# Gate pairs: high parts of the weight blocks first, weight sums in SBUF, gate tiles in two places by turns, all spatial products in the first pair

## The reference

```python
mq, mk, mv, mo, mi, mf, su, sv, wq, wk, wv, gl = split_in(h @ p['w_in'])
...
y_sg, v_norm = spatial_gating(su, sv, ...)      # u * (w_spatial @ layer_norm(v) + b)
...
gates = jax.nn.sigmoid(gl).reshape(B, S, N_BRANCH, D_MODEL)
merged = (gates[:, :, 0] * (y_ml @ p['w_br_mlstm'])
          + gates[:, :, 1] * (y_sg @ p['w_br_gmlp'])
          + gates[:, :, 2] * (y_sw @ p['w_br_swa']))
x = x + g1 * rms_norm(merged @ p['w_out'], p['g_post_mix'])
```

## Time and profile before

| | |
|---|---|
| median of three runs | 2094.71 us |
| profiled execution, its span | 2096.62 us, 2094.8 us |
| PE busy | 2031.4 us (97%) |
| PE weight load busy | 1956.9 us (93%) |
| DVE, ACT, POOL busy | 1088.8, 685.9, 1025.6 us |
| mean granted TensorE clock | 0.990 |
| HBM traffic | 100 GB/s over the span |
| chain that ended last | PE 84%, DVE 5%, issue 3%, DMA 3% |

### The profile page before, as it was taken

How to read it: one execution, slowest core, us unless ns; L and a number is a source line. 1 busy time by engine, 2 the same in 40 slices (tenths; PEclk the granted TensorE clock), 3 DMA queues, 4 the chain that set the end, 5 groups by cost and what they waited for, 6 DMA issues and landing times.

```text
span 2094.8 us, 38683 instructions
## 1 busy us (share of the span) xinstructions
PE 2031.4 (97%) x16121; PEld 1956.9 (93%) x16121; DVE 1088.8 (52%) x1769; ACT 685.9 (33%) x1476; POOL 1025.6 (49%) x552
## 2 busy tenths in 40 slices
PE   8999999998999999999999999999899999999998
PEld 7999898997899999999999989889889999999998
DVE  5222466455456626557563245662645573647473
ACT  4111224123334333325532111431233344525253
POOL 0444454653473745453735445446437646354543
PEclk9999999998999999999999999999999999999999
DMA  9746221222351343233544342222223413222332
GB/s 360 248 136 61 67 76 51 74 71 61 87 184 51 121 131 86 86 92 89 173 127 163 61 66 77 61 60 75 61 71 104 169 31 96 82 85 84 98 89 79
DMA packets 300093, 211.94 MB, mean 101 GB/s; under 512 B 14048, under 2 KB 294160, under 8 KB 296720
## 3 DMA queue, kind: packets, MB, share of 16 engines
q1 hardware_dynamic: 293168, 205.94, 34.1%
q10 hardware_dynamic: 6752, 3.53, 0.7%
HBM read 204.65 MB, written 4.07 MB: 100 GB/s over the span
## 4 chain that ended last, share of the span: by engine, by line
PE 84%; DVE 5%; issue 3%; DMA 3%; POOL 2%; ACT 2%; SPq 0%; DVEq 0%; ACTq 0%; POOLq 0%
PE ps L1060 32%; PE ps L1152 19%; PE ps L1088 13%; PE ps L1779 3%; PE ps L1172 3%; DMA raw<-in_w_in 2%; PE ps L1178 1%; PE ps L1305 1%; PE ps L1220 1%; DVE t_sum L2538 1%; PE ps L1520 1%; PE ps L1684 1%; PE ps L1647 1%; PE ps L1535 1%; PE ps L1662 1%
## 5 line engine op out<-in xcount | busy, mean ns | idle before, releaser
L1060 PE MATMUL ps<-h_hi,hi_lo 128*128 128x288 f32 x2560 | 463.0, 299 | 0.3 <-POOL hi_lo L959 0.2
L956 POOL TENSOR_TENSOR hi_lo<-raw,consts 128x1024 fp32r<-128x1024 f32 (+1 forms) x112 | 218.6, 1951 | 447.4 <-PE ps L1060 319.2
L1060 PEld LDWEIGHTS ps<-h_hi,hi_lo 128*128 128x128 f32 x2560 | 380.5, 189 | 8.0 <-issue 5.3
L987 POOL TENSOR_TENSOR a_lo<-raw,a_hi 128x512 fp32r<-128x512 f32 x108 | 160.2, 1484 | 271.8 <-ACT a_hi L2363 271.8
L959 POOL TENSOR_TENSOR hi_lo<-raw,hi_lo 128x1024 fp32r<-128x1024 f32 (+1 forms) x112 | 274.7, 2452 | 8.8
L1060 PE MATMUL ps<-h_lo,hi_lo 128*128 128x288 f32 x1280 | 274.4, 296 | 0.0
L1060 PEld LDWEIGHTS ps<-h_lo,hi_lo 128*128 128x128 f32 x1280 | 206.4, 189 | 0.0
L1088 PE MATMUL ps<-yf_hi,fo_h 128*128 128x288 f32 x704 | 152.5, 298 | 3.0 <-DVE yf_lo L2538 3.0
L1088 PE MATMUL ps<-yf_hi,fo_l 128*128 128x288 f32 x704 | 151.0, 296 | 0.0
L1088 PE MATMUL ps<-yf_lo,fo_h 128*128 128x288 f32 x704 | 150.7, 296 | 0.0
L956 POOL TENSOR_TENSOR hx<-raw,consts 128x1024 fp32r<-128x1024 f32 x26 | 53.1, 2044 | 149.5 <-PE ps L1178 65.5
(11 more groups left out here) (448 smaller groups left out, 5113.5 us busy)
## 6 DMA issues: line engine op xcount, KB each, us to landing
ada<-in_w_ada SPq DMA_DIRECT2D x23, 2048.0 KB, 9.4
raw<-in_w_in SPq DMA_DIRECT2D x88, 512.0 KB, 3.8
raw<-in_w_ffn_in SPq DMA_DIRECT2D x144, 256.0 KB, 3.1
raw<-in_w_ffn_out SPq DMA_DIRECT2D x32, 384.0 KB, 3.4
raw<-in_w_in SPq DMA_DIRECT2D x40, 256.0 KB, 3.4
raw<-in_w_ffn_out SPq DMA_DIRECT2D x32, 320.0 KB, 3.2
raw<-in_w_out SPq DMA_DIRECT2D x16, 512.0 KB, 3.9
raw<-in_w_ffn_in SPq DMA_DIRECT2D x16, 512.0 KB, 3.8
```

The lines of the kernel that those rows point to most:

```text
L956: pool.tensor_tensor(hi, RAW[s][:, 0:size], ONES[:, 0:1].to_broadcast([128, size]), ALU.mult).then_inc(chunk_hi, 1)
L987: pool.tensor_tensor(lo[:, :], RAWB[o], hi[:, :].bitcast(f32), ALU.subtract).then_inc(s_alo, 1)
L1060: m = pe.matmul(o[:, h, :], a[:, k, c0:c0 + 128], mv(k, h), start=(k == 0 and begins), stop=(k == nk - 1 and a is wl))
```

## The change

1. The order of the spatial products: z2 and z3 follow branch tiles 0 and 1 of b = 1 directly. The data sums begin earlier: two ahead of z2 and z3 on DVE, the others around the merges of tiles 2 and 3.
2. The weight sums s1, s2 and s4 lie in SBUF, each in the place of its own low part (s3 keeps its place). s2 needs no low part of s1 any more, s4 none of s2; instead each sum of a pair waits until the pair before has used that low part.
3. ACT rounds the three blocks ahead of the four sums.
4. The sums of pair 0 stand ahead of, and between, the last merges of the plain gates.
5. The gate tiles go by turns to `tmp` (pairs 0, 2, 4) and `sq` (pairs 1, 3). The first copy of a pair waits for the merges of the pair before the last.

The core of the diff:

```diff
-Z_AFTER = {0: (0, 1), 2: (2, 3)}
+Z_AFTER, Z_LATE = {0: (0, 1)}, {0: (2, 3)}
...
+        if _b_ == 1:
+            MIX += [f"z{_i}" for _i in Z_LATE.get(_n, ())]
...
-                    [(f"g_{o}_{x}", [128, WH], f32r) for o in ("a11", "s1", "s2", "a12") for x in ("hi", "lo")])
+                    [(f"g_{o}_{x}", [128, WH], f32r) for o in ("a11", "s1", "s2", "a12") for x in ("hi", "lo")],
+                    [("pad_g0", [128, 3 * WH], f32), ("g_s1_sum", [128, WH], f32), ("pad_g1", [128, WH], f32),
+                     ("g_s2_sum", [128, WH], f32)])
+        GSUM = {i: r[f"g_s{i}_sum"] for i in (1, 2)}
...
+                    [("pad_g4", [128, WH], f32), ("g_s4_sum", [128, WH], f32)])
+        GSUM[4] = r["g_s4_sum"]
...
-        GTILES = [(SQ[:, 0, :], SQ[:, 1, :]) if bn == (2, 6) else (TS[:, 0, :], TS[:, 1, :]) for bn in GPAIRS]
+        GTILES = [tuple(x[:, e, :] for e in range(2)) for x in (TS, SQ)]
...
-                    if i == 0 and GPAIRS[p] != (2, 6):
-                        b, m = GPAIRS[p][0], GPAIRS[p][1] - 2
-                        if m < 0:
-                            b, m = b - 1, 6
+                    if i == 0 and p != 1:
+                        b, m = GPAIRS[p - 2] if p else (1, 2 * PLAIN1 - 2)
...
-                    zs = Z_AFTER.get(n, ())
                     gate(1, n)
-                    if zs:
-                        z_bias(zs[0])
+                    if n == 0:
+                        z_bias(0)
+                    elif n == 2:
+                        gt_high(0, T1H[:, :, :], T1SUM[:, :, :])
                     else:
+                        gt_high(2, T4H[:, :, :], T4SUM[:, :, :])
+                    gate(1, n + 1)
+                    if n == 0:
+                        z_bias(1)
+                        for g in range(4):
+                            act.wait_ge(unit_of(l, f"z{g}"), read(l, f"z{g}"))
+                            y_hi(4 + g, WQ[:, 2 + g % 2, :])
+                            if g < 2:
+                                z_bias(2 + g)
+                    elif n == 2:
                         gt_high(1, T2H[:, :, :], T2SUM[:, :, :])
-                    gate(1, n + 1)
-                    if zs:
-                        z_bias(zs[1])
-                    for g in zs:
-                        act.wait_ge(unit_of(l, f"z{g}"), read(l, f"z{g}"))
-                        y_hi(4 + g, WQ[:, 2 + g % 2, :])
-                    if 3 in zs:
-                        gt_high(0, T1H[:, :, :], T1SUM[:, :, :])
-                gt_high(2, T4H[:, :, :], T4SUM[:, :, :])
                 gt_high(3, T3H, GT3SUM[:, :, :])
                 act.wait_ge(o_stored, l * (16 * O_STORES) + 16 * O_STORES)
-                for o in ("a11", "a12"):
+                for o in ("a11", "a12", "a22"):
                     gate_block_high(o, 0)
-                for i in (1, 2, 3):
+                for i in (1, 2, 3, 4):
                     gate_sum_high(i, 0)
-                gate_block_high("a22", 0)
-                gate_sum_high(4, 0)
...
                     elif p + 1 < NGP:
                         for o in ("a11", "a12"):
                             gate_block_high(o, p + 1)
-                        for i in (1, 2, 3):
+                    gate_tanh(2, p)
+                    if p + 1 < NGP:
+                        gate_block_high("a22", p + 1)
+                    if p + 1 < NGP and not close:
+                        for i in (1, 2, 3, 4):
                             gate_sum_high(i, p + 1)
-                        gate_block_high("a22", p + 1)
-                        gate_sum_high(4, p + 1)
                 act.wait_ge(o_stored, l * (16 * O_STORES) + 16 * O_STORES)
                 for k in MERGED:
...
                 def gate_weights(i, p):
-                    n, bank = l * NGP + p, gate_sum(l, p)
+                    n = l * NGP + p
+                    if p:
+                        dve.wait_ge(g_prod, gate_product(n - 1, {1: "p5", 2: "p6", 3: "p7", 4: "p3"}[i]))
                     if i == 1:
                         dve.wait_ge(g_raw["a21"], 16 * (n + 1))
                         dve.wait_ge(g_raw["a22"], 16 * (n + 1))
-                        dve.wait_ge(unit_of(l, f"ga{p}"), empty(l, f"ga{p}"))
-                        x = bank, RAWB["a21"], RAWB["a22"], ALU.add
+                        x = RAWB["a21"], RAWB["a22"], ALU.add
                     elif i == 2:
                         dve.wait_ge(g_raw["a11"], 16 * (n + 1))
-                        dve.wait_ge(g_lo, 4 * n + 1)
-                        x = bank, bank, RAWB["a11"], ALU.subtract
+                        dve.wait_ge(g_sum, 4 * n + 1)
+                        x = GSUM[1][:, :], RAWB["a11"], ALU.subtract
                     elif i == 3:
-                        if p:
-                            dve.wait_ge(g_prod, gate_product(n - 1, "p7"))
-                        x = GS3SUM[:, :], RAWB["a11"], RAWB["a21"], ALU.subtract
+                        x = RAWB["a11"], RAWB["a21"], ALU.subtract
                     else:
                         dve.wait_ge(g_raw["a12"], 16 * (n + 1))
-                        dve.wait_ge(g_lo, 4 * n + 2)
-                        x = bank, RAWB["a12"], bank, ALU.subtract
-                    tt(*x).then_inc(g_sum, 1)
+                        dve.wait_ge(g_sum, 4 * n + 2)
+                        x = RAWB["a12"], GSUM[2][:, :], ALU.subtract
+                    tt(GSUM[i][:, :], *x).then_inc(g_sum, 1)
                 def gate_weights_low(i, p):
-                    dve.wait_ge(g_hi, 4 * (l * NGP + p) + i)
+                    n = l * NGP + p
+                    dve.wait_ge(g_hi, 4 * n + i)
+                    if i < 3:
+                        dve.wait_ge(g_sum, 4 * n + 2 * i)
                     hi, lo = GOPND[f"s{i}"]
-                    tt(lo[:, :], GS3SUM[:, :] if i == 3 else gate_sum(l, p), hi[:, :].bitcast(f32), ALU.subtract).then_inc(g_lo, 1)
+                    tt(lo[:, :], GSUM[i][:, :], hi[:, :].bitcast(f32), ALU.subtract).then_inc(g_lo, 1)
...
                 for n in range(0, 2 * PLAIN1, 2):
-                    zs = Z_AFTER.get(n, ())
-                    for g in zs:
...
-                    if 3 in zs:
+                    for g in Z_AFTER.get(n, ()):
+                        spatial_gate(g)
+                    if n == 2:
+                        whole(2, T1SUM[:, :, :], 0, 0)
+                        less(3, T1SUM[:, :, :], GT3SUM[:, :, :], T1SUM[:, :, :])
+                        whole(4, T2SUM[:, :, :], 1, 1)
+                    elif n == 4:
+                        gate_weights(1, 0)
+                        gate_weights(2, 0)
+                        gate_weights(3, 0)
+                        gate_weights_low(1, 0)
+                    merge(1, n)
+                    if n == 0:
                         whole(0, GT3SUM[:, :, :], 0, 1)
-                        whole(1, T1SUM[:, :, :], 0, 0)
-                        less(2, T1SUM[:, :, :], GT3SUM[:, :, :], T1SUM[:, :, :])
-                    merge(1, n)
-                    if 3 in zs:
-                        whole(3, T2SUM[:, :, :], 1, 1)
-                        less(4, GT3SUM[:, :, :], T2SUM[:, :, :], GT3SUM[:, :, :])
+                    elif n == 2:
+                        less(5, GT3SUM[:, :, :], T2SUM[:, :, :], GT3SUM[:, :, :])
+                        less(6, T2SUM[:, :, :], T2SUM[:, :, :], T1SUM[:, :, :])
+                    else:
+                        gate_weights(4, 0)
+                        gate_weights_low(2, 0)
                     merge(1, n + 1)
-                    if 3 in zs:
-                        less(5, T2SUM[:, :, :], T2SUM[:, :, :], T1SUM[:, :, :])
-                        whole(6, T4SUM[:, :, :], 1, 0)
+                    if n == 0:
+                        whole(1, T4SUM[:, :, :], 1, 0)
+                    elif n == 2:
                         less(7, T4SUM[:, :, :], T4SUM[:, :, :], T2SUM[:, :, :])
                         gt_low(0, T1L[:, :, :], T1SUM[:, :, :], T1H[:, :, :])
                         gt_low(1, T2L[:, :, :], T2SUM[:, :, :], T2H[:, :, :])
-                gt_low(2, T4L[:, :, :], T4SUM[:, :, :], T4H[:, :, :])
-                gate_weights(1, 0)
-                gate_weights_low(1, 0)
+                        gt_low(2, T4L[:, :, :], T4SUM[:, :, :], T4H[:, :, :])
+                    for g in Z_LATE.get(n, ()):
+                        spatial_gate(g)
+                gate_weights_low(3, 0)
                 gt_low(3, T3L, GT3SUM[:, :, :], T3H)
-                gate_weights(2, 0)
-                gate_weights_low(2, 0)
-                gate_weights(3, 0)
-                gate_weights(4, 0)
-                gate_weights_low(3, 0)
                 gate_weights_low(4, 0)
...
                     gate_weights(1, p + 1)
+                    gate_weights(2, p + 1)
+                    gate_weights(3, p + 1)
                     gate_weights_low(1, p + 1)
-                    gate_weights(2, p + 1)
+                    gate_weights(4, p + 1)
```

(7 more changed lines are left out.)

46 lines of the change are left out of this document (21 added, 25 removed).

## The result

The changed kernel takes 2062.28 us (median of 4 runs, 2061.19 to 2063.65), beside 2094.41 us for the kernel before on the same chip (4 runs, 2093.65 to 2095.01). The ratio is 0.9847, 95% interval 0.9830 to 0.9864, and 32.1 us are gone. The profiled execution's span is 2061.9 us against 2094.8 before, 32.9 us less. The forecast was 2058.3, its range 2050 to 2071.

A forecast was written before the change was run, and what follows sets the result against it. TensorE's lost time in the pair regions, 44.0 us, was taken as the bound; adding 0.6 and leaving 4.1 a layer (2.4 + 0.8 + 0.5 + 0.4) saves 36.4 us: 2058.3 us, range 2050 to 2071.

The forecast's parts named there:

- What bounds the kernel: TensorE's idle and low-clock time in the two pair regions: 22.7 and 21.3 us lost, 44.0 together.
- Steady pairs at nothing: Pairs 1 to 4: sums and first copy arrive before TensorE needs them, so no wait, costed at nothing.
- the cover: Steady pairs: time by which sums and copies come ahead of TensorE's need, 2.5 to 3.5 us.
- Early branch weights: With a22 rounded first, the branch weights are loaded 9 us earlier than 485.10.
- Pair 0: p6 still waits for the first copy behind both merges, 2.4 us a layer; p5 finds its low part.
- Low clock: Slow matmuls behind the p6 wait of pair 0: half of 1.6 us, so 0.8 us a layer.
- p3's wait for s4: Pair 0: p3 needs the low part of s4, up to 2.0 us late; taken as 0.5 us.
- Branch split: Spatial products: splitting branch tiles 2 and 3 beside one plain gate, 0 to 2.4 us; taken as 0.4 a layer.
- The sum: Whole kernel: 44.0 + 0.6 - 2 x 4.1 = 36.4 us saved, giving 2058.3 us.
- Rival B: Steady pairs still wait because POOL's low parts and split hold DVE: 2073.5 us; chance 17%.
- Rival D: First copy stays held behind the rounding of s4, only the waits for p5 go: 2085 us; chance 4%.

The follow-up runs named there:

- run 1: Changed kernel with the gate tiles of pairs 0 to 3 all in `tmp` again: 2077.95 us.
- run 12: Kernel before with only the new orders (spatial products, data sums, start of pair 0, s3 and s4 ahead of the first merge, a11 and a12 rounded earlier): 2078.9 us.
- run 11: Kernel before with gate tiles by turns, and a22 rounded ahead of the sums in every pair but pair 4: 2083.6 us.
- run 6: Changed kernel, but in pair 3 ACT makes its third copy ahead of rounding s1 of pair 4: 2058.84 us.
- run 2: Changed kernel, but ACT rounds a22 behind the sums s1, s2, s3 again: 2062.71 us.
- run 5: Changed kernel, but in pair 0 both merges stand ahead of s4 and the low parts, and ACT's first copy ahead of rounding s4: 2059.65 us.
- after: The changed kernel itself, with all five parts of the change: 2062.28 us.
- run 8: Changed kernel, but POOL fills the low parts of a11, a12 and a22 with zeros in place of computing them: 2055.22 us.
- run 9: Kernel before with the gate tiles by turns and nothing else: 2089.91 us (11 runs).

## Why the prediction was right, point by point

- **What bounds the kernel** held. All of the gain in the span but 0.1 us lies in the two regions; 44.0 us were lost there and 11.3 are left, where I had 7.4 (8.2 less the split, which is ahead of them).
- **Steady pairs at nothing** held in pairs 1, 2 and 4: no idle row. DVE lost 3.3 us to POOL in pair 1, and the cover was not used up: the low part of s2 is there at 495.89, 2.5 us before the matmul at 498.41 that asks for it, since the sums had begun 1.5 us earlier than I had it (488.47, with the pair before ending at 489.0). In pair 3 the step failed. I wrote that pair 4's sums "are made during pair 3 as before, and PE did not wait there before". PE had not, because p6 waited for the merges first: in runs 1 and 12, where it still does (2.0 to 2.2 us in pair 3), p7 does not wait. With that tie gone the next wait in ACT's order showed, 0.78 and 1.34 us. It is the tie to the merges that hides it and not any wait at p6: in run 11 p6 of pair 3 waits for the rounding of s4 (0.87 and 2.12 us), and p7 waits as well. This is the term that I missed; mending it is worth 3.4 us (run 6).
- **Early branch weights**: 9.4 us earlier, as forecast, but for another reason than the one I gave. Rounding a22 first neither is needed (run 2) nor suffices (run 11). DVE's s3 held the same blocks, and I had not followed it.
- **Pair 0**: p6 waited 2.41 and 3.03 us for 2.4. DVE's row for the low part of s1 took 1.75 us beside POOL, one collision of 1.1 us where I had added 0.8 in all; p5 found its part. The cause, two merges ahead of the copy, held (run 5).
- **Low clock**: 1.6 and 2.1 us for 0.8. The term was half of what was measured. Windows of after, layer 0, behind the idle of 2.41 us:

```profile
478.00:481.00 3.00, 1.60 (x7) 1.63 (x8) 2.98 (x3) 0.82 (x2) 1.78 (x1) 0.69 0.80 238
481.00:484.00 3.00, 3.00 (x19) 3.00 (x19) 3.00 (x2) 0.41 (x1) 2.92 (x2) 0.74 0.00 0
```

The second has 19 matmuls in 3 us where full speed has 22.5 (3 / 0.1332). In layer 1 the first ten matmuls behind the idle of 3.03 us are at full speed and the low clock comes only then. This is the first slow row; the starts behind it are 0.24 us apart until 1492.84:

```profile
1489.48 0.44 PE L1782 MATMUL ps<-t_hi,g_s_hi 128*128 128x288 f32 x1
```

- **p3's wait for s4** (0.5 a layer) did not occur, although DVE's row for the low part of s4 took 2.87 us at 482.26. It ended at 485.13, 1.0 us behind the 484.1 that I had, where the wait at p6 is already counted. But the low clock had set the matmuls back by 1.6 us, and the one that asks for it starts at 485.67. So this term came out at nothing by a delay that I had too small elsewhere.
- **Branch split** (0.4 a layer): the row at 447.80 waits 0.16 us. Two of the four waits for the spatial products went, 0.6 us, as forecast. Outside the regions no change is left on balance, though the first input's DMA cost PE 2.7 us in this execution and 1.2 before, so terms of this size can't be read there.
- **The sum**: 36.4 forecast, 32.1 measured. In the regions 3.8 us more are left than I had, by these rounded terms: 0.6 at p6, 2.1 at p7 of pair 3 and 2.1 of low clock, less 1.0 at p3. Outside them I had 0.2 lost (0.6 less 0.8) and 0.1 was won. The remaining 0.8 lie between the spans (32.9) and the medians (32.1). That the forecast is only 4.0 us off is in part luck: 4.8 us were missing from my terms and 1.3 were too many.
- **Rival B** is half right in its mechanism: DVE is stretched from 0.69 to 1.8 us three times in most of pairs 1 to 3, and in pairs 1 and 2 it cost PE nothing. In pair 3 and pair 0 it may have: in run 8, where those rows are not stretched, the waits at p7 of pair 3 are gone and those at p6 of pair 0 are 1.05 and 0.55 us shorter. The Trainium skill's rule ("SBUF — State Buffer", section "Who interferes with whom") speaks of GpSimd instructions that read SBUF; run 8 agrees on that point, 0.69 us beside fills and 1.79 beside subtractions.
- **Rival D** was dismissed for a wrong reason. I had read "the copy is released by the merge alone" off; a releaser is only the last of several, and in run 9 the next one, the rounding of s4, came 0.5 us ahead of the copy. It got 4% on that reading. What kept it from coming true is that the change also makes s4 early, by its place ahead of the merges and by the new start of pair 0. My walk through a steady pair used that order, and I gave it no price of its own.

So the number was right within its range by a reading that took the change as a whole. Its account of what makes the branch weights early was wrong, and it had no price for each part.

What stays open: how the 7.1 us of run 8 divide between collisions and shorter POOL work, what the order of s3, s4 and the first merge is worth by itself, and why the clock falls in layer 1 only ten matmuls behind the idle of 3.03 us.

## What to carry to other kernels

A wait in the profile names the last of its guards. Before costing its removal, follow the second, on the same engine's order and on the buffers, and ask which later wait the present one hides: here the second guard was the rounding of s4, whose end the old trace already showed 1.3 us ahead of the copy, and the hidden wait was a copy behind a rounding in pair 3. Test parts both ways, undone from the new kernel and done alone on the old. Undone, the turns were worth 15.7 us; alone, 4.1. And read the whole difference of such a kernel to the old one: what I took for pair 0's order held a new order in pairs 1 to 3 too.

## What the runs showed of the hardware that I had not expected

- The rule was in what I expected of run 8, the sizes are new. A fill on POOL runs beside a DVE instruction with two SBUF inputs at no cost to it (0.69 us inside a fill of 1.06), where a subtraction on POOL makes the same one 1.79. Both pay: POOL's three subtractions took 4.87 us for 3.8 in the changed kernel.
- Idle times of about the same length in the same place did not cost the same in clock. Layer 0 of after idles 2.41 us at p6 and loses 1.6 us to the low clock; in run 6 it idles 2.50 us at the same matmul, and its region of 77.55 us is 2.45 over the floor, so it loses nothing. Layer 1 of run 6 idles 3.18 us in all, 3.01 of it at p6, and is 5.3 over the floor (80.38), so 2.1 us are low clock.
